# The mixer of a hybrid decoder step in another order: S5 scan beside the projections, gates, GLU and S5 output as half tiles between attention steps

## The reference, cut to what matters

```
h = h + 0.5 * ffn1(rms(h))                      # D_FF 2816, D_MODEL 1024
u = rms(h) ; proj = u @ w_in                    # S5 input 512, c_q 384, c_kv 256, k_r 32, g_a 1024, g_b 1024
ys = S5(a_in)                                   # diagonal complex recurrence over time, 2048 states
z = gelu(ys) ; y_a = (z * sigmoid(z @ w_glu + b)) @ w_a_out
o = attention in latent space: prompt causal over 512 keys (8 heads);
    the 32 new tokens over 4096 cached rows each (32 pages of 128 rows per request) and themselves
y_b = o @ w_b_out
h = h + (sigmoid(g_a) * y_a + sigmoid(g_b) * y_b) @ w_out
h = h + 0.5 * ffn2(rms(h)) ; y = rms(h) * g
```

## Time and profile before

| | |
|---|---|
| median of 3 runs | 1509.96 us (1507.07 to 1513.16) |
| the profiled execution | 1512.59 us, of which the span in the trace is 1510.7 us |
| first projection tile of the mixer | 449.1 us |
| first prompt step (units 0 to 3 are done) | 631.5 us |
| last values of a prompt step | 846 us or so |
| first tile of w_out, first tile of FFN2 | 1029.3 us, 1077.4 us |
| PE busy | 92% of the span |
| mean granted clock | 0.966 |

### The profile page before, as it was taken

The page is one execution under the profiler, slowest core; times in us unless marked ns, Lnnn a source line. Parts: engine busy times, 40 slices in busy tenths (PEclk is TensorE's granted clock), DMA queues, the critical chain, the costliest instruction groups (busy, mean ns, idle before and its releaser), DMA issues.

```text
span 1510.7 us, 28473 instructions
## 1 busy us (share of the span) xinstructions
PE 1391.1 (92%) x11800; PEld 1268.8 (84%) x11800; DVE 611.9 (41%) x950; ACT 416.4 (28%) x672; POOL 373.1 (25%) x385
## 2 busy tenths in 40 slices
PE   6999998999989987988888789999999999999995
PEld 6999998999979974444444689999999999999994
DVE  5234334233254766333333454444523332332324
ACT  5232211221242200422223342223422222222223
POOL 3218253246221163422220000001121021021023
PEclk9999999999999986998999899999999999999998
DMA  5222222223132143798896022222222322322211
GB/s 214 79 77 98 78 76 72 93 59 103 58 110 81 32 143 116 263 311 296 295 320 261 28 70 85 84 84 87 82 89 64 112 77 68 106 77 77 98 48 67
DMA packets 72450, 175.22 MB, mean 116 GB/s; under 512 B 9506, under 2 KB 10435, under 8 KB 72291
## 3 DMA queue, kind: packets, MB, share of 16 engines
q1 hardware_dynamic: 70306, 169.69, 33.8%
q0 software_dynamic: 2048, 4.20, 0.9%
HBM read 170.85 MB, written 3.00 MB: 115 GB/s over the span
## 4 chain that ended last, share of the span: by engine, by line
PE 73%; DVE 10%; ACT 5%; DMA 4%; issue 2%; SPq 2%; POOL 2%; DVEq 0%; ACTq 0%; POOLq 0%
PE d L1304 63%; SPq L294 2%; DVE w_lo L847 2%; ACT w_hi L418 2%; PE e L1477 2%; DVE x_lo L852 1%; PE e L1500 1%; DMA kv_raw<-kv_src 1%; PE d L1574 1%; DMA kv_w<-kv_src 1%; DMA kv_hl<-kv_src 1%; PE d L1584 1%; DVE rstd L857 1%; PE e L1480 1%; DVE h L886 1%
## 5 line engine op out<-in xcount | busy, mean ns | idle before, releaser
L847 DVE TENSOR_TENSOR w_lo<-raw,w_hi 128x1024 fp32r<-128x1024 f32 (+2 forms) x200 | 231.3, 1157 | 634.7 <-ACT w_hi L418 634.5
L1304 PE MATMUL d<-x_hi,w_hi 128*128 128x272 f32 x1824 | 383.5, 292 | 21.9 <-DVE w_lo L847 10.9
L1304 PE MATMUL d<-x_hi,w_lo 128*128 128x272 f32 x1824 | 380.0, 290 | 0.0
L1304 PE MATMUL d<-x_lo,w_hi 128*128 128x272 f32 x1824 | 379.1, 289 | 0.0
L418 ACT CAST w_hi<-raw 128x1024 fp32r<-128x1024 f32 (+2 forms) x200 | 191.2, 958 | 525.9 <-PE d L1304 525.7
L1304 PEld LDWEIGHTS d<-x_hi,w_hi 128*128 128x128 f32 x1824 | 289.3, 190 | 26.6 <-DVE w_lo L847 11.1
L1304 PEld LDWEIGHTS d<-x_lo,w_hi 128*128 128x128 f32 x1824 | 289.6, 190 | 0.0
L1304 PEld LDWEIGHTS d<-x_hi,w_lo 128*128 128x128 f32 x1824 | 287.9, 191 | 0.0
L680 POOL TENSOR_TENSOR hid<-silu,up 128x544 f32<-128x544 f32 x44 | 59.7, 1357 | 505.5 <-DVE up L875 505.1
L1304 PE MATMUL d<-hid_hi,w_hi 128*128 128x272 f32 x704 | 149.9, 295 | 16.3 <-DVE h L886 13.7
L1304 PE MATMUL d<-hid_hi,w_lo 128*128 128x272 f32 x704 | 147.4, 291 | 0.0
(11 more groups left out here) (304 smaller groups left out, 1576.0 us busy)
## 6 DMA issues: line engine op xcount, KB each, us to landing
raw<-w_gu SPq DMA_DIRECT2D x88, 512.0 KB, 3.4
kv_w<-kv_src SPq DMA_DIRECT2D x80, 256.0 KB
kv_raw<-kv_src SPq DMA_DIRECT2D x72, 256.0 KB
kv_hl<-kv_src SPq DMA_DIRECT2D x72, 256.0 KB
raw<-w_post SPq DMA_DIRECT2D x34, 512.0 KB, 3.5
raw<-w_d1b SPq DMA_DIRECT2D x16, 384.0 KB, 3.2
raw<-w_d2b SPq DMA_DIRECT2D x16, 384.0 KB, 3.2
raw<-w_in SPq DMA_DIRECT2D x10, 512.0 KB, 3.5
```

Source lines behind the costliest of these rows:

```text
L847: nc.vector.tensor_tensor(w_lo[:, s % 2, 0:n, :], raw[:, s % NRAW, 0:n, :], w_hi[:, s % 2, 0:n, :].bitcast(FP), ALU.subtract).then_inc(S.l ...
L1304: ins = mm(d[:, par, b, 0:HALF], w[:, pos, c0 + k, :], x[:, k, b * HALF:(b + 1) * HALF], start=first, stop=stop)
```

## The change

- **S5 first.** `w_in` runs in the order S5 input, c_q, key, latent rows. The scan's chunks stand between those ten tiles and the eight query tiles: `chunk_inputs` after tiles 2, 4, 7 and 9, `outputs` after tile 8, after query tiles 1 and 4, and after the last. `hprev`, `s_rot` and the scan's buffers are smaller, in other places.
- **No early units.** All 32 units stand in the 32 steps; unit n is in step n.
- **Half tiles.** Gates (32), GLU (8) and S5 output (16) become `job`s: one half of the tokens, 24 or 12 matmuls into the one bank `e[:, 3]`, evacuated before the next job. Steps 0 to 20 have two jobs (n even) or one (n odd) of the gates, steps 23 to 26 two of the GLU, steps 28 to 31 one of the S5 output; the other twelve stand in the tail, between the parts of the joining chain.
- **DRAM.** h is written to DRAM before the projections and read back after the last step (2.2 MB each way). Each raw gate block (278 KB, 16 of them) is written by ACT's queue and read back by SP into a ring of three when it is used.
- **Page ring.** Pages have 20 places instead of 24 in three units. When the values of unit n are done, SP starts the second half (4 pages) of unit n+2 and then the first half of unit n+3.
- **FFN start.** Tile 0 of the down projection gets its last chunk before tile 1 gets its second half of chunks; `s5_matrices` is moved one or two tiles later.

The tail also loses eight scalings on DVE (a matrix `sel` takes them in), and the two FFNs are as before otherwise.

```diff
-EARLY, LATE = 4, 27
+RING = 20
+    def jobs(n):
+        if n < 22:
+            return list(range((3 * n + 1) // 2, min(J_GLU, (3 * n + 4) // 2)))
+        if n < 23:
+            return []
+        if n < 27:
+            return [J_GLU + 2 * (n - 23), J_GLU + 2 * (n - 23) + 1]
+        if n < 28:
+            return []
+        if n < 4 * H:
+            return [J_A + n - 28]
+        return list(range(J_A + 4, JOBS))
 # SP
+        for n in range(4 * H):
+            sp.wait_ge(S.un_pv, n + 1)
+            if n + 2 < UNITS:
+                half_unit(n + 2, 1)
+            if n + 3 < UNITS:
+                half_unit(n + 3, 0)
+            for k in jobs(n):
+                if ends_slot(k):
+                    post(job_slot(k) + 4)
...
+        sp.wait_ge(S.s_pe, 4 * H)
+        load(h[:, :, :], h_kept, S.h_in)
 # ACT
+        def job_end(k):
+            if k < J_GLU and k % 2 == 1:
+                act.wait_ge(S.hj_evac, k + 1)
+                i = k // 2
+                nc.scalar.dma_start(gates[i], gate_m[:, i % NG, :]).then_inc(sem["gate_out%d" % (i % NG)], 16)
...
+            if ends_slot(k):
+                split_hi(job_slot(k) + 2, k + 1, sem_free=S.hj_done)
 # DVE, ten projection tiles
+            if i == 2:
+                forward(0)
+            if i == 3:
+                scan(0)
+            if i == 4:
+                backward(0)
+                forward(1)
+            if i == 5:
+                scan(1)
+            if i == 6:
+                backward(1)
+            if i == 7:
+                inverse(N_Q, rq)
...
+                forward(2)
 # PE, ten projection tiles
+            if i == 6:
+                column_sums(N_Q, 0, (S.fwd_done, 2))
+            if i == 7:
+                pe.wait_ge(S.rms_done, N_Q + 1)
+                chunk_inputs(2)
 # PE, a job and the steps
+            pe.wait_ge(S.lo_done, s + 1)
+            if k >= 1:
+                pe.wait_ge(S.hj_evac, k)
+            for c in range(nk):
+                for w, x in ((w_hi, xh), (w_hi, xl), (w_lo, xh)):
+                    ins = mm(e[:, 3, 0:HALF], w[:, s % 2, c0 + c, :], x[:, c, half], start=c == 0 and x is xh and w is w_hi,
+                             stop=c == nk - 1 and w is w_lo)
+            ins.then_inc(S.hj_done, 1)
         for n in range(4 * H):
             scores(n)
+            unit_turn(n)
+            if n + 1 < UNITS:
+                unit_scores(n + 1)
+            for k in now[:1]:
+                job(k)
             if n >= 1:
                 turn(n - 1)
+            unit_values(n)
             if n >= 2:
                 values(n - 2)
+            for k in now[1:]:
+                job(k)
             if i == 0 and hd + 1 < H:
                 keys(hd + 1)
 # PE, FFN
-                for r in range(2):
+                for r, ks in ((0, range(nb - 1)), (1, range(nb // 2))):
...
-                for r in range(2):
-                    products(r, r, 0, nb, hid_hi, hid_lo, ks=[nb - 1], **hid_in).then_inc(S.tile_done, 1)
+                products(0, 0, 0, nb, hid_hi, hid_lo, ks=[nb - 1], **hid_in).then_inc(S.tile_done, 1)
+                products(1, 1, 0, nb, hid_hi, hid_lo, ks=range(nb // 2, nb)).then_inc(S.tile_done, 1)
```

More of the change, by code:

```diff
@@ L166, in build @@
[L166 to L179, removed]
+    ckv = inside("ckv", [LC, TOK], FP, rh, 2048 + 4 * T4, RH)
+    krope = inside("krope", [TOK], FP, rh, 2048 + 6 * T4, RH)
@@ L369, in _ @@
+        post(S_G)
+        post(S_G + 1)
+        sp.wait_ge(S.bwd_done, UC)
+        load(w_ukt[0:NOPE, :, :], a["w_ukt"], S.ukt_in)
+        sp.wait_ge(S.h_done, UC)
+        load(a["ssm_p"], h_fin[:, :, :], S.stores)
+        load(w_uv[:, :, :], a["w_uv"], S.vw_in)
         sp.wait_ge(S.kvn_done, LC)
@@ L372, in _, with half_unit @@
         load(a["krope_out"], krope[0:ROPE, :], S.kept)
-        unit(2)
-        for v in range(3, EARLY + 1):
-            unit(v)
-        sp.wait_ge(S.h_done, UC)
-        load(w_uv[:, :, :], a["w_uv"], S.vw_in)
+        post(S_G + 2)
+        table = {}
+        def half_unit(v, half):
+            if half == 0:
+                _, table[v] = nc.values_load_multi_w_load_instructions(pt_sb[0:1, v * UNIT:(v + 1) * UNIT], (mybir.EngineType.SP,),
+                                                                       min_val=0, max_val=POOL - 1,
+                                                                       skip_runtime_bounds_check_because="VectorE clamped the table")
+            wraps = v * UNIT % RING + UNIT > RING
+            for i in range(GRP):
+                g = GRP * (half != wraps) + i
+                load(kv[:, kv_place(v, g), :], a["kv_src"][bass.ds(table[v][g], 1)].rearrange("a p n -> p (a n)"), sem["unit_in%d" % (v % NKV)])
@@ new lines, in _ @@
+        for n in range(4 * H):
[7 more added lines that the diff above has]
+                    post(job_slot(k) + 4)
+            if n == 27:
+                for r in range(NG):
+                    reload(r)
+                sp.wait_ge(S.g_ready, UC)
+                load(w_uv2[:, :, :], a["w_uv"], S.uv2_in)
+            if n in (29, 31):
+                reload(NG + (n - 29) // 2)
@@ new lines, in _ @@
+        sp.wait_ge(S.s_pe, 4 * H)
+        load(h[:, :, :], h_kept, S.h_in)
+        r = NG + 2
+        for k in jobs(4 * H):
+            if k % 2 == 1:
+                reload(r)
+                r += 1
+            if ends_slot(k):
+                post(job_slot(k) + 4)
+        post(S_OUT + 2)
+        post(S_OUT + 3)
+        for r in range(r, 2 * KC):
+            reload(r)
+            if r == 2 * KC - 4:
+                post(S_OUT)
+            if r == 2 * KC - 2:
+                post(S_OUT + 1)
@@ L399, in _ @@
+        for s in range(S_OUT + 4, S_FFN2):
             post(s)
@@ L625, in _ @@
+        branch_gate(KC)
         act.wait_ge(S.kept, 32)
-        def gates(t):
-            for x in range(2):
-                act.wait_ge(S.evac, t + x + 1)
-                nc.scalar.activation(gate_m[:, x, :], gate_m[:, x, :], ACT.Tanh, scale=0.5).then_inc(S.gate_done, 1)
         def merged_hi(m):
@@ L1526, in _ @@
-        new_values(1)
-        unit_turn(0)
-        unit_scores(1)
-        unit_values(0)
-        outputs(0)
-        outputs(1)
-        for v in range(1, EARLY):
-            unit_turn(v)
-            unit_scores(v + 1)
-            unit_values(v)
-            if v + 1 < UC:
-                outputs(v + 1)
-        pe.wait_ge(S.vw_in, 32)
-        pe.wait_ge(S.y_out, UC)
-        for k in range(4):
-            for c in range(LC):
-                ins = mm(d[:, k // 2, k % 2, :], ckv[:, c, k * P:(k + 1) * P], w_uv[:, c, :], start=c == 0, stop=c == LC - 1)
-            ins.then_inc(S.vp_pe, 1)
+        pe.wait_ge(S.y_out, 3)
@@ L1545, in keys @@
+        outputs(3)
         def keys(hd):
```

1233 lines of the change are left out of this document (650 added, 583 removed).

## The result

The changed kernel takes **1570.8 us** (median of 4, 1563.2 to 1572.9) where the kernel before takes 1510.4: a ratio of 1.040, 95% interval 1.036 to 1.043. It is slower by 60 us, and 58 over the forecast of 1512.6, outside its range. The profiled execution took 1570.45 with a span of 1568.7; the forecast span was 1513.3.

What follows compares the result with a forecast made beforehand. PE is near full in the FFNs, so only the mixer's waits, at most 100 us, can be won. Order +6.6, clock +6 and FFNs -10 gave +2.6 on a span of 1510.7: 1512.6 us as median, range 1479 to 1547.

Steps and rivals of the forecast that it cites:

- part 5: TensorE clock in the page loop: +6 us, bounds 0 and 15, the latter if it stays at 0.94.
- My own sign: Expected in the changed trace: a clock near 0.9 or more in the loop.
- My third rival: The clock falls in the loop, half clock for a third of each step's work: +15 to +25, 1530; chance 0.12.
- L: Page loop: time from a unit's values until the released half unit's 4 pages land, 5.6 us, between 4.2 and 7.2.
- part 1: Projections with the S5 scan, to the first step: scores(0) 140 us after tile 2, at 611 instead of 631.5.
- the tail with its tiles: After the last values: 37 us for twelve jobs and joining chain, then 73 for eight tiles and w_out.
- my own price: Late pages in the loop: each 0.1 us more of L costs 2.5 us.
- the late half unit: Rival for the loop: L is 7.2, 24 steps lose 1.6, +38, so 1550; decides from L 5.8; chance 0.17.
- The steps' structure: The 32 steps: page waits of 3 to 4 us after blocks 1 and 3, none after 0; steps 13.1, 11.85, 12.1, 12.3.
- my fourth rival: DVE in order in part 1: two more waits of 4 to 5, query stage at half clock, +12, 1525; chance 0.1.
- FFNs: Part 6, down projections in both FFNs: the new tile order shortens waits for h, -10 us.
- The prize is at most 100 us: Mixer: PE's work is about 528 us in 628, so at most 100 can be won.

Runs made afterwards that it cites:

- run 5: The changed kernel again, unedited, on the chip of three later runs: 1571.2 us, ratio 1.043 to the kernel before.
- the filler kernel: Changed kernel with 12 useless matmuls on constants between unit_turn and unit_scores in steps behind one without a job b: 1553.1 us, ratio 1.031.
- the filler: Kernel of run 13 with 16, 6 and 8 matmuls on constants in the waits ahead of query tiles 6, 7 and ukt: 1463.3 us, ratio 0.970.
- scans and norms: Scans of S5 chunks 1 to 3 over 2 of 8 rows, on unit_values-first order: ratio 0.978; kv norms behind last query, on run 13's kernel: 0.972.
- The orders above: Changed kernel with unit_values ahead of unit_scores and jobs around them: 1486.1 us; with run 11's turn order: 1483.0; with two tail banks too: 1481.2, repeated 1468.4.
- run 11: Changed kernel with unit_values ahead of unit_scores, plus unit_turn ahead of scores and the prompt's turn behind unit_scores without a first job: 1483.0 us, ratio 0.971.
- runs 2, 3 and 8: Changed kernel: 2, job a before unit_scores in even steps, 1539.8 us; 3, quarter-size page loads, 1513.7 us; 8, as 2 with SP's weight posts later, ratio 1.009.
- run 13: Changed kernel with unit_values ahead of unit_scores, two banks for tail jobs and run 11's turn order, repeated on another chip: 1468.4 us, ratio 0.974.
- run 10: Changed kernel with unit_values ahead of unit_scores, tail jobs writing in turn to two banks: ratio 0.977.

## Why the prediction was wrong, point by point

**The step that failed is part 5, the clock.** I read that the loop before kept 0.94 with waits of 2.5 in steps of 6.5, and took +6 with 15 as the bound. The bound itself was false: 0.94 came with waits of 2.9 us at most, and I carried it to waits of 3 to 5 us. Behind most of these TensorE is at half speed, in the step above for 5.5 us, and the loop's clock is 0.90. By the traces this costs 31 us in the loop, 25 more than the +6; the filler kernel, with most of the low clock gone, was 18 us faster. My own sign, a clock near 0.9 in the loop, did not fit the +6: if 0.94 costs 15, 0.90 costs 25. My third rival said just this, at half clock for a third of each step's work, and I gave it a price of 15 to 25 and a chance of 0.12. The row that should have raised both was in front of me: 0.63 at 561 to 587 us. The Trainium skill (TensorE: Matmul & The Clock Gate, the part on thin M) describes tiles that start at the low clock because each waits for a transfer; the trace agrees: in run 5, 17 of the loop's 30 unit_scores took over 1.7 us, all behind waits for pages.

The clock is the largest miss, but not all of it. Of the loop's +34 it is some 25, and L some 11 by its price (next point); part 1 adds 15 and the tail with its tiles 7. With the clock right and nothing else the forecast would have been some 1538, still 33 too low.

**L was right in kind and too low.** From the values' end to a unit_scores that waited for pages it is 5.4 to 6.5 in 21 of 23 steps, 6.8 and 7.2 in two, and 6.1 in the mean, for 5.6. By my own price of 2.5 us for each 0.1 this is some 11 us, and it lies beyond the 5.8 at which I had the late half unit decide. In the first 20 steps the waits sum to 44.4 us where mine were 37.5, and with the last eleven to 72.1. With a quarter of the bytes it was near 3.6. The Trainium skill (DMA: Bandwidth & Descriptors, Anatomy of one DMA) gives its 2.0 us plus bytes over 436 GB/s for one transfer that GpSimd issues; taken for these four loads of SP, as I took it, L would be 4.6, an estimate. The trace does not agree: the fourth load is issued 1.8 us after the first and lands some 3.6 later.

**The steps' structure was right.** Waits after blocks 1 and 3, next to none after 0, steps after block 0 of 13.2 for 13.1. Moved work lies beside the pages only where it stands between the release and the next use. In the changed kernel job a stands behind that use in every step.

**Part 1 was short by 15.** The waits for m_sum, the root and krope came as 7.3, 1.8 and 3.2 for my 5.4, 3.2 and 3.3. Not in my sum were 4.7 for qparts, 2.3 ahead of ukt and 1.2 for s_fwd: with the others 9 of the 15. The remaining 6 I put to the low clock from 560 us on (0.79); that is argued, as the filler gave only 2.2 back. That DVE in order holds the stage (my fourth rival) was tested twice, with scans and norms, and neither moved the end by over 1.5: its waits are there, but the time won at one was lost behind it.

**Tail and tiles were short by 7.** I reckoned 1.5 for a job and 0.6 behind it. From one start to the next it is 2.4 at the full clock (1062.0 to 1064.4) and 3.7 at the low one (1044.9 to 1048.6). The clock of the tail is 0.84, but here no long wait stands ahead of the low stretch. It follows c_olat, 32 narrow matmuls in 4.4 us behind a wait of 0.86:

```profile
1040.69 4.41 PE L1783 MATMUL e<-sel,o_n 128*128 128x32 f32 x32 [0.86 <-DVE sel L1386]
```

```profile
1045.00:1050.00 5.00, 4.38 (x19) 4.09 (x19) 1.98 (x4) 0.00 (x0) 0.00 (x0) 0.50 0.11 15
```

What brought the clock down there, no run tells.

**FFNs were right**: -12.0 for -10, alone -8.4 on the kernel before.

**"The prize is at most 100 us" was not put to the test.** The orders above got 40 to 45 us of it against the kernel before, from the change's own parts.

## What to carry to other kernels

When work is moved beside transfers, look where it stands between the release of a buffer and its next use, not at how much there is in a step: by the order of a step the same instructions were 4% slower or 1.4% faster than the kernel before, and with the turns in another order too (11) 2.9% faster. Price waits like these, of 3.6 to 5.0 us on TensorE, twice, once for themselves and once for the work behind them: here 72 us of waits cost another 31. If a stretch cannot be reordered, a filler that ends before the data lands tells what the clock costs, but measure one of its matmuls first.

## What the runs showed of the hardware

- In the changed kernel's two traces unit_scores took 1.63 us behind every wait for pages of 2.1 and less, 1.63 to 2.94 behind those of 2.4 to 3.5, and 2.27 to 2.95 behind all of 3.6 to 5.0. In the other orders a shorter wait did not always leave the clock alone: in runs 2, 3 and 8 unit_scores took 1.93 to 2.66 behind four waits of 1.9 to 2.1.
- A filler matmul of 128 columns on constants took 0.23 us in a row of 22 (5.08 us), with two records in the trace for each, where the four of unit_turn, with one record each, take 0.61 in all, 0.15 each.
- On two of the chips, TensorE stood idle for stretches of 0.2 to 1.0 us, put down to issue, (4.1 to 4.8 us in all) among the matmuls of outputs 3, between 590 and 602 us, and the first unit_scores came at 626 to 628 where it came at 614 to 617 on the others. In run 11 the 64 matmuls on hprev took 10.3 us where run 13 has 2.1, and w_uv's 16 behind them 9.2 where it has 7.1; in run 10 the clock from 600 to 605 us was 0.50. The kernel before was slower on the same two chips, by some 17 us over its whole length. What it is, no run here tells.
